# An up projection in three 256-column matmuls a tile, on one core of Trainium2

## The reference

```python
def conv_ffn(h, w_up, w_conv, b_conv, w_down):
    up = h @ w_up                        # (256, 2048) @ (2048, 11264)
    up = lax.conv_general_dilated(up, w_conv[:, None, :], window_strides=(1,),
                                  padding=[(CONV_WIDTH - 1, 0)], ...,
                                  feature_group_count=C) + b_conv   # width 3, causal, per channel
    u, g = jnp.split(up, 2, axis=-1)
    return (jax.nn.gelu(g) * u) @ w_down # (256, 5632) @ (5632, 2048)
```

## Time and profile before

| | |
|---|---|
| time, median of three runs | 1585.43 us |
| three runs | 1583.99 to 1590.58 us |
| span of the profiled execution | 1587.5 us |
| PE busy | 1496.3 us, 94% |
| DVE busy | 1115.7 us, 70% |
| ACT busy | 759.4 us, 48% |
| DMA | 364.71 MB, mean 230 GB/s |

### The profile page before, as it was taken

How to read it: one execution, slowest core, us unless ns; L and a number is a source line. 1 busy time by engine, 2 the same in 40 slices (tenths; PEclk the granted TensorE clock), 3 DMA queues, 4 the chain that set the end, 5 groups by cost and what they waited for, 6 DMA issues and landing times.

```text
span 1587.5 us, 23241 instructions
## 1 busy us (share of the span) xinstructions
PE 1496.3 (94%) x8062; PEld 1289.3 (81%) x8062; DVE 1115.7 (70%) x1259; ACT 759.4 (48%) x795; POOL 80.0 (5%) x170
## 2 busy tenths in 40 slices
PE   3559999999999999999999999999999999999997
PEld 3557888888888888887878888888888887888886
DVE  6977888888888777777558666666666666445444
ACT  1125454545454434434367566655665565443442
POOL 3000101011111111010000000000000000000000
PEclk9999999999999999999999999999999999999999
DMA  9996888888889898988535655565556554555551
GB/s 348 345 344 204 276 256 274 260 276 260 278 265 304 290 303 286 298 283 322 199 128 164 211 180 181 167 211 184 182 163 210 185 184 160 191 198 193 187 183 53
DMA packets 259674, 364.71 MB, mean 230 GB/s; under 512 B 11296, under 2 KB 210466, under 8 KB 259123
## 3 DMA queue, kind: packets, MB, share of 16 engines
q1 hardware_dynamic: 240112, 294.69, 56.6%
q0 software_dynamic: 18432, 67.12, 12.7%
q10 hardware_dynamic: 1090, 2.40, 0.4%
HBM read 362.06 MB, written 2.10 MB: 229 GB/s over the span
## 4 chain that ended last, share of the span: by engine, by line
PE 82%; DMA 9%; DVE 5%; issue 2%; ACT 1%; SPq 1%; DVEq 0%; POOLq 0%; ACTq 0%
PE ps L1148 82%; DMA ada<-in_w_ada 5%; DMA raw<-in_w_ada 3%; DVE acc L714 2%; DVE ws L702 1%; SPq L294 1%; DVE acc L765 1%; DMA raw<-in_w_in 1%; ACT ws L418 0%; PE ps L1296 0%; DVE yt L1058 0%; DVE yo L1058 0%; ACT tmp L563 0%; DVE x L1064 0%; ACT yt L613 0%
## 5 line engine op out<-in xcount | busy, mean ns | idle before, releaser
L1148 PE MATMUL ps<-hT,ws 128*128 128x512 f32 (+1 forms) x4896 | 875.4, 340 | 3.1 <-DVE ws L702 2.5
L1148 PEld LDWEIGHTS ps<-hT,ws 128*128 128x128 f32 x4896 | 751.4, 189 | 115.7 <-DVE ws L702 3.2
L702 DVE TENSOR_TENSOR ws<-raw,ws 128x2048 fp32r<-128x2048 f32 x245 | 558.7, 2288 | 192.7 <-ACT ws L418 192.4
L418 ACT ACTIVATE ws<-raw 128x2048 fp32r<-128x2048 f32 x245 | 465.7, 1910 | 225.4 <-PE ps L1148 191.0
L1148 PE MATMUL ps<-ws,asp 128*128 128x512 f32 x1056 | 241.5, 391 | 3.2 <-DVE up L1108 2.1
L1148 PEld LDWEIGHTS ps<-ws,asp 128*128 128x128 f32 x1056 | 199.3, 189 | 45.3 <-DVE up L1108 2.6
L714 DVE SCALAR_TENSOR_TENSOR acc<-ada,scol,acc 128x1024 f32<-128x1024 f32 x120 | 153.7, 1281 | 51.0 <-DMA ada<-in_w_ada 49.5
L1148 PE MATMUL ps<-ws,hT 128*128 128x512 f32 (+1 forms) x896 | 180.4, 361 | 1.7 <-DVE mods L720 1.7
L1148 PEld LDWEIGHTS ps<-ws,hT 128*128 128x128 f32 x896 | 150.1, 188 | 27.3 <-issue 1.7
L640 ACT ACTIVATE cv<-up,cols 128x256 f32<-128x256 f32 x88 | 48.2, 594 | 124.0 <-DVE up L1108 124.0
L405 POOL DMA_DIRECT2D ada<-in_w_ada x128 | 67.7, 529 | 636.7 <-DVE acc L714 404.0
(11 more groups left out here) (181 smaller groups left out, 780.4 us busy)
## 6 DMA issues: line engine op xcount, KB each, us to landing
raw<-in_w_up SPq DMA_DIRECT2D x176, 512.0 KB, 4.5
raw<-in_w_in SPq DMA_DIRECT2D x162, 512.0 KB, 5.3
ada<-in_w_ada POOLq DMA_DIRECT2D x128, 512.0 KB, 4.8
raw<-in_w_down SPq DMA_DIRECT2D x88, 512.0 KB, 4.4
raw<-in_w_ada SPq DMA_DIRECT2D x64, 512.0 KB, 7.4
raw<-in_w_o SPq DMA_DIRECT2D x32, 512.0 KB, 5.5
raw<-in_w_gla_out SPq DMA_DIRECT2D x16, 512.0 KB, 5.4
raw<-in_w_moba_out SPq DMA_DIRECT2D x16, 512.0 KB, 5.3
```

What stands on the lines that cost most here:

```text
L418: act.activation(ws[:, slot, :, 0, :], raw_blocks(slot), ACT.Copy).then_inc(hi, 1)
L702: dve.tensor_tensor(ws[:, slot, :, 1, :], raw_blocks(slot), ws[:, slot, :, 0, :].bitcast(F32), ALU.subtract).then_inc(done, 1)
L1148: return pe.matmul(out_, lhsT, rhs, start=start, stop=stop)
```

## The change

`weights_still` is replaced in the up projection alone by a new function, `up_still`, which issues three matmuls of 256 columns for each block and tile, all into the first half of the bank. ACT then copies that half of both banks straight to `up`, and the addition on DVE and the semaphore `cross5` are gone. Copied, split and convolved data are the same as before.

```diff
-        cross5, up_ready, cb_done, conv_g, gelu_done, conv_done = sems("cross5 up_ready cb_done conv_g gelu_done conv_done")
+        up_ready, cb_done, conv_g, gelu_done, conv_done = sems("up_ready cb_done conv_g gelu_done conv_done")
...
                 act.wait_ge(used4, 4 * i + W_UP + n - 2)
                 act.wait_ge(conv_done, q + 2)
-                act.activation(cv[:, :, :], ps[:, 2 * g:2 * g + 2, TOK:], ACT.Copy).then_inc(cross5, 1)
+                act.activation(up[:, :, 2:], ps[:, 2 * g:2 * g + 2, 0:TOK], ACT.Copy).then_inc(up_ready, 1)
                 act.wait_ge(up_ready, q + 1)
...
                     q = 2 * i + g
-                    dve.wait_ge(cross5, q + 1)
-                    dve.tensor_tensor(up[:, :, 2:], ps[:, 2 * g:2 * g + 2, 0:TOK], cv[:, :, :], ALU.add).then_inc(up_ready, 1)
                     for ct in range(2):
...
+            def up_still(slot, k0, bank, used, before=None):
+
+                for k in range(8):
+                    kk = k0 + k
+                    if before:
+                        before(kk)
+                    for ct in range(2):
+                        cs = slice(P * ct, P * (ct + 1))
+                        o = ps[:, bank + ct, 0:TOK]
+                        mm(o, ws[:, slot, k, 0, cs], hT[:, kk, 0:TOK], kk == 0, False)
+                        mm(o, ws[:, slot, k, 0, cs], hT[:, kk, TOK:], False, False)
+                        last = mm(o, ws[:, slot, k, 1, cs], hT[:, kk, 0:TOK], False, kk == KT - 1)
+                last.then_inc(used, 1)
...
                     pe.wait_ge(split4, 4 * i + W_UP + n - 2)
-                    weights_still(SLOT4[n], hT, 8 * (n % 2), KT, 2 * (n // 2), used4, h_is_ready if n < 2 else None)
+                    up_still(SLOT4[n], 8 * (n % 2), 2 * (n // 2), used4, h_is_ready if n < 2 else None)
```

## The result

The changed kernel takes 1598.41 us (median of nine runs, 1594.71 to 1600.56), the kernel before, run beside it, 1589.70. The ratio is 1.0067 with a 95% interval of 1.0041 to 1.0093: 10.7 us slower, between 6.5 and 14.8; the two medians by themselves are 8.7 us apart. The forecast was 1591.2 us with a range of 1577 to 1617, and +5.8 us, within the 0.5% that it called no change. The time lies in the range and moved the way that was forecast, but by 0.67%, over that bound. The two traces by themselves differ by 5.6 us in span (1593.1 against 1587.5), and 1593.1 is nearly the 1593.3 that the sum gave for the span.

A forecast was written before the change was run, and what follows sets the result against it. The prediction took PE, which never waits inside the up loop, to bound the kernel. Its terms +9.6 - 2.1 - 1.7 = +5.8 us, set against 1585.43 us, gave 1591.2 us, range 1577 to 1617.

The forecast's parts named there:

- What bounds the stage: Up projection loop: PE never waits, so work taken from DVE and ACT gains nothing there.
- Start to start of a matmul: Up projection: three matmuls of 256 take 360 ns instead of 353.2 for the pair, 1408 times: +9.6 us.
- The bound that tempted: Up projection: 117 ns for each 256, 350 ns for three; as faster rival -8.3 us, 1577.1 us, 12%.
- The slow rivals: Up projection: surcharge grows with matmul count; three take 370 ns (+19.8 us, 30%) or 379 ns (1617.9 us, 12%).
- The end: End of up projection: PE's wait for the addition goes, -2.1 us, and the low clock behind it, -1.7 us.
- The total: Whole kernel: +5.8 us on 1585.43 us gives 1591.2 us; the profiled span of 1587.5 becomes 1593.3 us.
- it stands 2.1 us above the median: Whole kernel: the profiled span of 1587.5 us lies 2.1 us above the median of 1585.43 us.

The follow-up runs named there:

- the repeated measurement: The changed kernel once more, unaltered, run against the kernel before: ratio 1.0067 (1.0035 to 1.0098).
- the first experiment: Kernel before, with ACT's copy and DVE's addition moved ahead of the two splits in the up stage's last turn: ratio 0.9963 (0.993 to 0.9995).

## Why the prediction was right

**What bounds the stage.** Right. The additions left DVE and the waits left ACT, PE stayed at 506.88 of 507 us, and nothing in the loop became faster. With the work put back on DVE and ACT the stage took the same 507.20 us.

**Start to start of a matmul.** Right: 120.0 ns, from two equations in rows of other stages, and confirmed for the down projection. That it fits to a tenth of a nanosecond is luck of rounding: the equations as they stand give 346.6 - 227.0 = 119.6. The term was +9.6 us and measured +9.25: 353.67 ns (497.97 / 1408) is the better figure for the pair over the whole stage than the 353.2 of one stretch, and the three of 256 took 360.2 (507.20 / 1408).

**The bound that tempted.** The distance of 117 ns behind a 256 was no cost. The variant with 128 columns shows how such a distance misleads. Its PE timeline in two short windows, first two matmuls of 128 in the array, then two of 256:

```profile
1101.40 0.34 PE L1146 MATMUL ps<-hT,ws 128*128 128x128 f32 x2
```
```profile
1101.57 0.45 PE L1146 MATMUL ps<-hT,ws 128*128 128x256 f32 x2
```

Less the 0.28 us that the second of each pair takes through the array, the starts stand 0.06 and 0.17 us apart, while the four take 0.46 us together. Only the sum over a repeating pattern is a cost.

**The slow rivals** (370 and 379 ns). Wrong: the surcharge of the strict turn doesn't grow with the number of matmuls. It vanishes when all have one length, falls to 348.6 ns a pair with two and two, and to 347.8 with sixteen and sixteen. Their premise, a surcharge of the up stage that the merge does without, was a reading of too few rows: the merge of the same trace has stretches at 353 ns too (the units at 613.23 above). Matmuls of two lengths are needed for it, but a change of length alone does not bring it, since the same turn also runs at 346.7 ns. What decides between the two rhythms, and what in PE makes them, is not shown.

**The end.** Right, -3.8 us forecast and -3.96 measured by itself: both the wait and the low clock behind it went. The early addition alone does the same.

**The total.** The sum was +5.8 us and the stretch shows +5.27, but the runs say +10.7 (6.5 to 14.8), and the time is 7.2 us above the 1591.2 that was forecast. The step that was too small is "it stands 2.1 us above the median": I tied the sum to the median of three runs, 1585.43, and the median of nine is 1589.70, 4.3 us higher. The other 2.9 us are the distance of the medians, 8.7, less the sum. Set against the traced run itself, at about 1589.1 us, the forecast would have been 1594.9, and the changed kernel's traced run took 1594.71. That this is so close is in part luck, since both executions reached the up stage at nearly the same time. The kernel before has a second, lower group of times, which the three runs shown at first and the trace don't tell apart. On the chip of the repeated measurement the changed kernel (1597.56) stands 7.0 us above the upper group's median of 1590.5 and 18.6 above the lower one's 1579.0. If the lower group ran its pairs in the merge's 346.7 ns, the changed kernel would stand 5.3 + 9.3 = 14.6 us above it. That fits in sign and nearly in size, and it fits that only the kernels with the strict turn have two groups and that every stretch of the merge runs at one of the two rhythms, but no trace of a lower-group run shows it.

## What to carry to other kernels

On an engine that never waits, work removed from others is worth only what stands at the stage's ends; look there first, and take that gain alone if it can be had (here by moving one copy and one addition). Count an added matmul of this type, with its load, at 13.3 ns even when the columns stay the same, and expect no less than 110 ns for one of 128 columns (nothing between 128 and 256 was run). Take such costs from sums over a whole pattern, never from one distance between starts; before a difference between two stages is called a property of one of them, read every stretch of the other. And look at all runs of a kernel before a forecast is tied to the median of three.

## What the runs showed of the hardware

- Matmuls of 512 and 256 columns in strict turn take 353.2 ns a pair or 346.6, at the same clock and with the same code. A stretch without a break keeps one of the two from end to end, and the same stretch can have the other in the next execution (5.66 and 5.55 us for 16 pairs above). Orders with longer runs of one length take 347.8 to 349.4 ns for the same columns.
- Two matmuls of 128 columns cost 110 ns each, like matmuls of one column, if the 256s beside them keep their 120 ns. A floor set by the load of the weights fits both.
- The Trainium skill (TensorE: Matmul & The Clock Gate, Back-to-back issue gap) has 2.5 ns of fixed cost for a single warm matmul. In this type, each matmul with its load, 13.2 to 13.4 ns were measured three times: at 512 columns ((239.61 - 0.39) / 1055 = 226.7 ns in the down projection of the first experiment), at 256 in the up stage and at 256 in the down projection.
- Of two pauses of PE 3 us apart, 1.05 and 2.14 us long, the first alone left the clock at 2.4 GHz, both together were followed by 3.5 us at 1.2 GHz. The second alone was not run.
